# Two-block transformer layer stack on one core: three weight tiles per contraction step at the head of each second-block layer

## The reference

```python
# second block, per layer l of 2
h = rms_norm(x, pre_norm_g[l])
proj = h @ w_in[l]                       # 2048 x 6656: 52 column tiles of 128
(rq, rk, rv, rg, dq, dk, dv, dg, lx, lg) = split(proj)
ret_out  = rms_norm(retention(rq, rk, rv)) * silu(rg)      # 6 heads of 128
lam      = exp(sum(q1*k1)) - exp(sum(q2*k2)) + lam_init    # from layer parameters
diff_out = rms_norm(diff_attention(dq, dk, dv, lam), g) * (1 - lam_init) * silu(dg)
lru_out  = rg_lru(conv(lx), ..., lru_lambda) * silu(lg)    # 6 tiles of 128
x = x + rms_norm(concat(ret_out, diff_out, lru_out) @ w_out[l], post_norm_g[l])
```

## Time and profile before

| what | us |
|---|---|
| median of three runs | 3411.26 |
| lowest and highest | 3410.83, 3414.91 |
| the profiled execution's own time | 3415.89 |
| its span, first to last instruction | 3414.0 |

### The profile page before, as it was taken

How to read it: one execution, slowest core, us unless ns; L and a number is a source line. 1 busy time by engine, 2 the same in 40 slices (tenths; PEclk the granted TensorE clock), 3 DMA queues, 4 the chain that set the end, 5 groups by cost and what they waited for, 6 DMA issues and landing times.

```text
span 3414.0 us, 43651 instructions
## 1 busy us (share of the span) xinstructions
PE 3176.8 (93%) x14102; PEld 2497.3 (73%) x14102; DVE 1807.2 (53%) x2314; ACT 1129.8 (33%) x2000; POOL 1307.2 (38%) x1005
## 2 busy tenths in 40 slices
PE   8999999999999997988999999989779999999895
PEld 6877777777777785866877777768667777777684
DVE  5867667544544315557365764451273756555413
ACT  5333333233333433333232223333332332333332
POOL 4433333333333343433433433334334434333344
PEclk9999999999999998988999999999899999999998
DMA  5322121122121421223322222132233222222322
GB/s 217 111 86 74 61 74 62 62 74 72 63 74 69 165 90 60 96 88 109 132 74 84 79 74 80 66 124 98 77 120 121 77 81 90 74 74 74 123 93 92
DMA packets 60424, 308.54 MB, mean 90 GB/s; under 512 B 5536, under 2 KB 5920, under 8 KB 28832
## 3 DMA queue, kind: packets, MB, share of 16 engines
q1 hardware_dynamic: 34992, 254.82, 21.0%
q10 hardware_dynamic: 25328, 52.37, 4.3%
HBM read 288.81 MB, written 18.35 MB: 90 GB/s over the span
## 4 chain that ended last, share of the span: by engine, by line
PE 65%; DVE 21%; DVEq 5%; issue 5%; ACT 2%; POOL 1%; ACTq 0%; DMA 0%; POOLq 0%
PE z L252 54%; DVE work L916 5%; PE scores L291 2%; DVE work L1046 2%; PE scores L375 1%; DVEq L1120 1%; PE o_bank L344 1%; DVE work L1035 1%; POOL w_low L215 1%; DVE work L910 1%; DVE work L974 1%; DVEq L1201 1%; DVE work L1182 1%; PE scores L325 1%; PE o_bank L310 1%
## 5 line engine op out<-in xcount | busy, mean ns | idle before, releaser
L215 POOL TENSOR_TENSOR w_low<-w_raw,w_high 128x512 fp32r<-128x512 f32 x968 | 1289.6, 1338 | 2077.9 <-ACT w_high L508 2067.2
L252 PE MATMUL z<-u_high,w_high 128*128 128x512 f32 x3744 | 1537.9, 411 | 87.8 <-DVE u_low L1167 38.3
L252 PE MATMUL z<-u_low,w_high 128*128 128x512 f32 x3744 | 1476.5, 394 | 0.0
L252 PE MATMUL z<-u_high,w_low 128*128 128x512 f32 x3744 | 1476.5, 394 | 0.0
L508 ACT ACTIVATE w_high<-w_raw 128x512 fp32r<-128x512 f32 x968 | 601.6, 628 | 1492.6 <-PE z L252 1454.5
L252 PEld LDWEIGHTS z<-u_high,w_high 128*128 128x128 f32 x3744 | 713.1, 190 | 300.4 <-issue 62.6
L252 PEld LDWEIGHTS z<-u_low,w_high 128*128 128x128 f32 x3744 | 714.2, 191 | 153.8 <-issue 13.4
L252 PEld LDWEIGHTS z<-u_high,w_low 128*128 128x128 f32 x3744 | 712.8, 190 | 154.8
L1182 DVE TENSOR_TENSOR work<-work 128x512 f32<-128x512 f32 x90 | 104.4, 1161 | 441.0 <-ACT work L688 427.1
L916 DVE RECIPROCAL work<-work 128x512 f32<-128x512 f32 x88 | 295.1, 3353 | 6.5
L910 DVE TENSOR_TENSOR work<-z,work 128x512 f32<-128x512 f32 x114 | 78.9, 692 | 182.8 <-PE z L252 173.0
(11 more groups left out here) (189 smaller groups left out, 2327.0 us busy)
## 6 DMA issues: line engine op xcount, KB each, us to landing
w_raw<-in_wt SPq DMA_DIRECT2D x243, 1024.0 KB, 4.7
out_hT<-work ACTq DMA_DIRECT2D x10, 1024.0 KB, 9.8
work<-in_xT ACTq DMA_DIRECT2D x8, 1024.0 KB, 12.5
work<-out_hT ACTq DMA_DIRECT2D x8, 1024.0 KB, 13.1
e_scratch<-work ACTq DMA_DIRECT2D x1, 4096.0 KB, 16.6
work<-e_scratch ACTq DMA_DIRECT2D x1, 4096.0 KB, 22.4
work<-in_gw ACTq DMA_DIRECT2D x2, 1792.0 KB, 11.8
work<-in_dec ACTq DMA_DIRECT2D x12, 256.0 KB, 2.6
```

Of the source, the lines that this page charges most:

```text
L215: pool.tensor_tensor(WL[:, 4 * q:4 * q + 4, :], RAW[:, t.odd, 512 * q:512 * q + 512].rearrange("p (k c) -> p k c", k=4), WH[:, 4 * q:4 * q ...
L252: mm = pe.matmul(bank[:], w[:, k, :], u[:, k, :], start=(k == 0 and n == 0), stop=(k == KT - 1 and n == 2))
```

## The change

- **Three tiles at once.** `three_tiles` takes the place of the first three `lx` tiles of each layer: for each contraction step k it waits for `u_ready` once and does nine products, three for each of tiles 0, 1 and 2, into Z[0], Z[1] and SC[0]. Tile 2 has WH and WL; the high and low parts of tiles 0 and 1 lie in a new view XW ("next_weights") over rows 16 to 31 of `work`. ScalarE fills it by `high_apart`, GpSimd by `low_parts_apart`, during the last two tiles of the stage ahead. Ahead of layer 0 these rows hold `e` of the gate tiles, so they wait for `pg_prod`.
- **The rest of the head.** Tiles 4 and 5 go to the banks of `turned`; the first two retention tiles may start with `behind=6`. The row sum stands after the second quarter of tile 4, and the root after ScalarE's third high part in that tile. In `squares`, the quarters of `high` are those of tile 3.
- **Parameters.** PR2 and DL hold both layers and are loaded at ScalarE's start. The arithmetic on them (`layer_params`, the same operations) stands in the output stage ahead: before the sum of squares on VectorE, before `out_slots` on ScalarE.
- **Loop.** The loop over the two layers is written out on all engines, with constants for the waits' values. A last extra weight load and split at the end of the program is gone.
- **Attention values.** The four contraction steps of both heads alternate between the heads, behind the waits for both copies.

```diff
+E_ROW = 16
...
+        work_at = nc.sbuf_base - ROWS * S * 4
+        XW = nc.alloc_sbuf_tensor_at("next_weights", [P, 16, S], F32R, offset=work_at + E_ROW * S * 4)
...
-        PR2 = sb("params_2", [P, PAR2])
+        PR2 = sb("params_2", [P, LAYERS, PAR2])
         LB = sb("lower_bounds", [P, 4, 8])
-        DL = sb("lambda_vectors", [P, 4, 64])
+        DL = sb("lambda_vectors", [P, LAYERS * 4, 64])
...
+        LX_BANK = {2: SC[0], 3: SC[1], 4: TP[0], 5: TP[1]}
+        XHI, XLO = (0, 8), (4, 12)
+
+        def four(r):
+
+            return XW[:, r, :].rearrange("p (k c) -> p k c", k=4)
...
+            def low_parts_apart(t, x, products=False):
+
+                for q in range(4):
+                    pool.wait_ge(sem("h_ready"), t.times(4, q + 1))
+                    if products:
+                        pool.wait_ge(sem("pg_prod"), 13 + q)
+                    pool.tensor_tensor(
+                        four(XLO[x] + q), RAW[:, t.odd, 512 * q:512 * q + 512].rearrange("p (k c) -> p k c", k=4),
+                        four(XHI[x] + q).bitcast(F32), ALU.subtract).then_inc(sem("l_ready"), 1)
 
...
-            with pool.Fori(0, NT // 2) as i:
+            with pool.Fori(0, T_L2 // 2) as i:
                 for o in range(2):
                     low_parts(Tile(o, (2, i)))
+            for l in range(LAYERS):
+                low_parts_apart(Tile(T_L2 + l * PER_LAYER), 0)
+                low_parts_apart(Tile(T_L2 + l * PER_LAYER + 1), 1, l == 0)
+                with pool.Fori(1, PER_LAYER // 2) as i:
+                    for o in range(2):
+                        low_parts(Tile(T_L2 + l * PER_LAYER + o, (2, i)))
...
+            def three_tiles(t, gen):
+
+                pe.wait_ge(sem("z_free"), t.times(1, -T_HGG))
+                for q in range(4):
+                    pe.wait_ge(sem("l_ready"), t.times(4, 8 + q + 1))
+                    for k in range(4 * q, 4 * q + 4):
+                        pe.wait_ge(sem("u_ready"), gen * 16 + k + 1)
+                        c = slice((k - 4 * q) * P, (k - 4 * q + 1) * P)
+                        hi = [XW[:, r + q, c] for r in XHI] + [WH[:, k, :]]
+                        lo = [XW[:, r + q, c] for r in XLO] + [WL[:, k, :]]
+                        for x, bank in enumerate((Z[0], Z[1], SC[0])):
+                            for n, (w, u) in enumerate(((hi, UH), (hi, UL), (lo, UH))):
+                                mm = pe.matmul(bank[:], w[x], u[:, k, :], start=(k == 0 and n == 0),
+                                               stop=(k == KT - 1 and n == 2))
+                    mm.then_inc(sem("w_free"), 3)
...
                     for hd in range(2):
                         pe.wait_ge(sem(f"pte{hd}"), PRIMED + j * 4 + a + 1)
-                        for c in range(4):
+                    for c in range(4):
+                        for hd in range(2):
                             mm = pe.matmul(OB[64 * hd:64 * hd + 64, a * P:(a + 1) * P],
                                            row(VN)[:, c * P + 64 * hd:c * P + 64 * hd + 64],
                                            row(PT + hd)[:, c * P:(c + 1) * P], start=(c == 0), stop=(c == 3))
...
-            with pe.Fori(0, LAYERS) as l:
-                base = l * PER_LAYER
-                for m in range(LRU_TILES):
+            for l in range(LAYERS):
+                three_tiles(Tile(T_L2 + l * PER_LAYER), l * 2 + 3)
+                for m in range(3, LRU_TILES):
                     for q in range(4):
-                        quarter(Tile(T_L2 + R_LX + m, (PER_LAYER, l)), q, l * 2 + 3 if m == 0 else None, SPARE.get(m))
-                    if m == 2:
-                        sum_rows(row(ACC), OB, (sem("sq_used"), PRIMED + l * 32 + 64), "ss_done")
-                step(Tile(T_L2 + R_RET, (PER_LAYER, l)))
+                        quarter(Tile(T_L2 + R_LX + m, (PER_LAYER, l)), q, None, LX_BANK[m])
+                        if m == 4 and q == 1:
+                            sum_rows(row(ACC), OB, (sem("sq_used"), PRIMED + l * 32 + 64), "ss_done")
+                step(Tile(T_L2 + R_RET, (PER_LAYER, l)), behind=(6, 6, 2, 2))
...
+            def high_apart(t, q, x):
+
+                act.wait_ge(sem("w_raw1" if t.odd else "w_raw0"), t.pair() * 16 + 16)
+                act.activation(four(XHI[x] + q),
+                               RAW[:, t.odd, 512 * q:512 * q + 512].rearrange("p (k c) -> p k c", k=4),
                                ACT.Copy).then_inc(sem("h_ready"), 1)
...
+                one(t.plus(14), 14, 0, n + 13)
+                if last == "three":
+                    for x in range(2):
+                        for q in range(4):
+                            high_apart(t.plus(16 + x), q, x)
+                    for q in range(3):
+                        high(t.plus(17), q, t.times(4, 60 + q + 1))
+                one(t.plus(15), 15, 1, n + 14, quarters=4 if last == "next" else 0)
+                if last == "three":
+                    high(t.plus(17), 3, t.times(4, 64))
                 inv_root(OB, row(ACC), D, (sem("ss_done"), ss), root)
...
+            for l in range(LAYERS):
+                act.dma_start(PR2[:, l, :], par2[l]).then_inc(sem("par_loaded"), 16)
+                act.dma_start(DL[:, 4 * l:4 * l + 4, :].rearrange("p a b -> p (a b)"),
+                              dlam[l].to_broadcast([P, 256])).then_inc(sem("par_loaded"), 16)
...
+            pg_slot(Tile(T_PG + 14), 14, 0, 32 + 13)
+            act.wait_ge(sem("pg_prod"), 8)
+            for q in range(4):
+                high_apart(Tile(T_L2), q, 0)
+            pg_square(14, 0, 15)
+            for q in range(4):
+                high_apart(Tile(T_L2 + 1), q, 1)
+            for q in range(3):
+                high(Tile(T_L2 + 1), q, 4 * T_L2 - 4 + q + 1)
+            pg_slot(Tile(T_PG + 15), 15, 1, 32 + 14, quarters=0)
+            high(Tile(T_L2 + 1), 3, 4 * T_L2)
+            pg_square(15, 1, 16)
...
-            with act.Fori(0, LAYERS) as l:
-                act.wait_ge(sem("par_used"), PRIMED + l)
-                act.dma_start(PR2[:], par2[l]).then_inc(sem("par_loaded"), 16)
-                act.dma_start(DL[:].rearrange("p a b -> p (a b)"), dlam[l].to_broadcast([P, 256])).then_inc(sem("par_loaded"), 16)
-                act.wait_ge(sem("par_loaded"), l * 32 + 32)
-                operand(Tile(T_L2, (PER_LAYER, l)), W[:, H:H + 16, :], PR2[:, G2_PRE:G2_PRE + 16], l * 16 + 16)
+            for l in range(LAYERS):
+                three = 4 * (T_L2 + l * PER_LAYER)
+                operand(Tile(T_L2, (PER_LAYER, l)), W[:, H:H + 16, :], PR2[:, l, G2_PRE:G2_PRE + 16], l * 16 + 16,
+                        weights=False)
                 act.wait_ge(sem("h_new"), l * 16 + 32)
...
-                squares(Tile(T_L2 + 1, (PER_LAYER, l)), l * 32 + 48)
+                squares(Tile(T_L2 + 2, (PER_LAYER, l)), l * 32 + 48, three + 3)
+                act.wait_ge(sem("w_free"), three + 12)
...
-                for m in range(2, LRU_TILES):
+                for m in range(3, LRU_TILES):
                     for q in range(4):
                         high(Tile(T_L2 + R_LX + m, (PER_LAYER, l)), q)
-                    if m == 2:
-                        inv_root(OB, row(RSTD), D, (sem("ss_done"), l * 2 + 4), "rstd_ready")
+                        if m == 4 and q == 2:
...
+                if l + 1 < LAYERS:
+                    layer_params(l + 1)
+                out_slots(Tile(T_L2 + R_OUT, (PER_LAYER, l)), l * 32 + 64, PR2[:, l, G2_POST:G2_POST + 16], l * 2 + 5, "root_ready",
+                          last="three" if l + 1 < LAYERS else "none")
...
+            def layer_params(l):
+
+                v.wait_ge(sem("par_loaded"), 32 * LAYERS)
+                for n in range(2):
...
+            layer_params(0)
...
-            with v.Fori(0, LAYERS) as l:
-                new_operand(l + 2, l * 32 + 48, v.to_reg(l * 64 + 64), PR2[:, G2_PRE:G2_PRE + 16])
-
...
+            for l in range(LAYERS):
+                new_operand(l + 2, l * 32 + 48, l * 64 + 64, PR2[:, l, G2_PRE:G2_PRE + 16])
+
...
-                v.tensor_scalar(SM[:, 62:63], SM[:, 61:62], 1.0, None, ALU.mult).then_inc(sem("par_used"), 1)
                 low(l * 32 + 64, MIX[:], a=8)
+                if l + 1 < LAYERS:
+                    layer_params(l + 1)
```

157 lines of the change are left out of this document (77 added, 80 removed).

## The result

The changed kernel takes 3367.62 us (median of 4 runs, 3365.44 to 3369.64), the kernel before in the same comparison 3412.01: a ratio of 0.9867, with a 95% interval of 0.9853 to 0.9880, or 44.4 us. The profiled execution takes 3365.44 us (span 3363.6), 50.4 us less than the profiled one of before. The forecast was 3364.

What follows compares the result with a forecast made beforehand. TensorE, busy 93% of the span, was taken as the bound, so only its gaps and low-clock stretches could be won: heads 34.4 plus attention values 12.6 make 47.0 us off the 3411.26 median, 3364; range 3355 to 3373 (8 in 10: 3343 to 3387).

Steps and rivals of the forecast that it cites:

- Tail: End of the stage ahead: ScalarE's longer queue delays D (VectorE's start on the new operand) 3.5 us, layer 1's root 2.4.
- Parameters: Head start: no 1.36 us DMA wait in layer 0; in layer 1 D 0.1 us behind the root, not 3.1.
- Three tiles: Layer heads: tiles end near D+38.7, VectorE bounds tile 8, turn at D+133.1; with tail and parameters 13.5 and 20.9 us gained.
- Attention values: Head pairs: alternating column halves save 0.6 us in each of 21 groups, 12.6 us; the eighth pair gains nothing.
- nothing overlaps now: Attention values: a group's 1.52 us means 0.19 per 128-column product, so the old order has no overlap.
- the first: Rival in attention values: column halves don't overlap, the 12.6 us is lost, 3377 us; chance 0.15.
- The second: Rival in the heads: VectorE not the bound at tile 8, tile 3's weights earlier, about 10 us more per layer, 3345; chance 0.15.
- The third: Rival in the heads: tile 3 and half of tile 4 at 1.2 GHz, up to 13.7 us a layer, 3382; chance 0.06.
- The fourth: Rival: low clock holds from D+3.6 to tile 4's third quarter, convolution 35.2 us later per layer, 3434; chance 0.02.
- fifth: Rival: ScalarE's queue or GpSimd's wait starts the three tiles some 20 us late a layer, within 0.2%; chance 0.02.

Runs made afterwards that it cites:

- the move of one order: Changed kernel with ScalarE's last exp (layer 0) or square (layer 1) ahead of the third tile's three high parts: 3361.30 us, ratio 0.9848 to the kernel before.
- parameters only: Kernel before plus parameters loaded at the start and computed a stage ahead, and the layer loop written out; nothing else: 3390.95 us against 3414.84.
- Root early: Changed kernel with the row sum right behind tile 3 and the root right behind tile 4's high parts: 3351.22 us, ratio 0.9813 to the kernel before.
- values only: Kernel before with only the attention-value products alternating between the two column halves: 3403.22 us against 3414.84, ratio 0.9971.
- head only: Changed kernel with the attention values issued half by half again, as before: 3376.32 us, ratio 0.9886 to the kernel before.
- all orders: Stores later plus the last exp or square ahead of the third tile's high parts: 3330.55 us, ratio 0.9760 to the kernel before.
- stores later: Root early, with ScalarE's stores of h moved from ahead of the squares to tile 4 and tile 3's high parts sooner: 3343.05 us, ratio 0.9786 to the kernel before.

## Why the prediction was right

The time, 3364 against 3367.6 and 3368.8 in two comparisons, came out by its own steps, but for the size of one term and for a gain that no term had:

- *Tail.* 3.5 us later in layer 0: stage end to D went from 11.6 to 14.5, so 2.9; the move of one order gave 2.2 of it back. In layer 1 the root was to be 2.4 later; from the stage end to the root it is 2.8 us longer (6.1 before, with D 3.1 behind the root; 8.9 now, with D 0.1 behind it).
- *Parameters.* D follows the root at once. In the kernel before, the trace has VectorE's branch back at 2449.06 and its next instruction at 2455.05, ScalarE's at 2451.69 and 2455.07, so the loop and not the parameters set the 3.1 us between root and D. The first `u_low` comes 3.75 us behind D in layer 0 and 2.7 in layer 1. The layers' D to turn went from 150.2 and 153.5 to 144.0 and 143.4 with the parameters alone. What the prediction didn't say is how much of the head's gain would remain without three tiles: over half (18.4 of 33.6 us in the heads).
- *Three tiles.* They start at D+4.6 and D+3.6 (3.6 forecast) and end at D+39.6 (38.7 forecast). The stores are issued at D+29.9 (29.5), tile 3's last quarter is ready at D+53.9 (52.5) and tile 3 ends at D+56.9 (56.2); the first convolution is at D+68.1 (67.3), the last read of tile 6 ends at D+107.3 (106.6), the wait before tile 8 is 6.0 (5), the turn is at D+133.9 and D+133.1 (133.1). Root early shows the bound to be the one named.
- *Attention values.* 21 groups x 0.6 = 12.6 was the one mis-sized term: it measured 9.6. A group saves 0.49, not 0.6, and the step that said "nothing overlaps now" was wrong, since in the old order the loads of the halves overlap already around their change (1.34 and not 1.70 us). That makes 10.3. The first group of a pair doesn't gain nothing, it loses 0.1: from where TensorE is free for it to the next instruction it takes 2.77 and not 2.70 us, which over seven pairs is most of the other 0.7. That the eighth pair gains nothing came out as forecast.
- *Not in the sum.* 4.0 us behind the turn of layer 1: from there to the end it takes 805.2 before, 807.3 with values only, 801.1 in the changed kernel, 801.3 with the head only and 800.2 with the parameters only. It seems to go with the loop over layers written out or with the parameters, and of the two I can't say which; TensorE's waits for VectorE in the steps of the heads are there 0.1 to 0.6 shorter each. But two kernels with both have 805.1 (root early) and 803.0 (all orders), so such a length alone is known to a few us only. There 104 and 99 products ran at the low clock, against 84 before and 82 in the changed kernel, so between these two it is not the clock.

By the profiled executions the terms make 13.3 + 20.5 for the heads (13.5 and 20.9 forecast) and 8.0 for the seven steps of the attention pairs, in one of which the changed kernel's clock fell (9.6 in an execution without that). The rest up to 50.4 is the 4.0, 1.5 in layer 0 and 3.0 ahead of and behind those steps, where no edit lies. So the two terms of the sum make 43.4 where 47.0 was forecast, and that the total still came within 4 to 5 us of the forecast owes something to gains that no step had: that is luck. Of the rivals, the first (halves don't overlap) falls with values only. The second (VectorE not the bound at tile 8) describes what root early and stores later had to make first. The third (a low clock in tile 3) is there in a small way: in layer 0, 6 products at 0.43 in the third quarter, hidden by the next wait, and in layer 1, 7 in the last quarter. The fourth and fifth did not happen: in the three tiles of layer 0, 9 products ran at the low clock.

## What to carry to other kernels

When an edit fills idle time of the busiest engine, write down which chain ends last afterwards: here the row sum, the root and six convolutions, which no tile of weights could make shorter, and moving two lines of order on that chain gave 16 to 18 us, a third of what the whole change gave. An order on one engine is cheap to try where the trace shows a wait of 13.8 us behind an operand that was ready long ago. Before you pack more work into a stage, ask what of the gain the simplest part brings alone.

## What the runs showed of the hardware

- Weight loads for different column halves (128x64 weights) run side by side when alternated: 16 in 0.85 us, the time of the 8 of one half alone. The group's start to the next instruction fell from 1.52 to 1.03 us. Two products of one half in a row cost little (0.90), a whole half in a row costs most of the overlap (1.34).
- VectorE's operations between SBUF buffers were longer where GpSimd computed low parts beside them: three table products of 128x512 took 1.89 us in a stretch without low parts and 2.95 in one with. So in these heads VectorE is faster while TensorE waits, and a convolution that starts 5.9 us later costs 3.5 us at the end.
- A loop's branch back cost VectorE 6.0 us and ScalarE 3.4 us from the branch to the next instruction (layer 1 of the kernel before). With the loop written out D follows the root by 0.1 us and not by 3.1.
- Executions differ by drops of the clock. In the profiled changed kernel one attention step took 61.0 instead of 59.4 us: behind a value group that had waited 1.75 us, eight products ran at 0.427 us (1.2 GHz). The other steps have the same wait and no drop. Over the seven steps, three kernels without a drop took 413.1 to 413.2 us and stores later, with three drops, 417.9.
